# Hybrid decoder step on one core: cached keys turned by VectorE, their strips and the convolution's weights on two DMA queues

## What is computed

```
a = rmsnorm(h);  [q k v | h B C] = a @ w_in            # 8 heads x 64, conv 512
q, k = rmsnorm per head
att: distances in three patterns (window, step): (128,1), (512,4), (2048,16)
     prompt: banded attention; sample: one softmax over the strided keys
             of the cache (2048 rows) and the new ones, + T5 bias by distance
conv: u = C*h;  y = B * (w0*u[t-2] + w1*u[t-1] + w2*u[t])
h += [rmsnorm(att) | rmsnorm(y)] @ w_out
h += MoE(rmsnorm(h))      # 4 groups x 8 experts, top 1 group, top 2 experts
h += (p @ w_proj) * sigmoid(rmsnorm(h) @ w_gate)
```

## Time and profile before

| | us |
|---|---|
| median of 3 runs | 1082.3 (1080.84 to 1082.81) |
| profiled execution | 1082.67 |
| its span, first to last instruction | 1080.7 |
| convolution stage in it | 280 to 498 |

### The profile page before, as it was taken

One profiled execution on the slowest core, in us unless ns is written; L12 is line 12 of the kernel. 1 busy time (PEld: TensorE's weight loads), 2 busy tenths in 40 slices (PEclk: granted clock), 3 DMA queues, 4 the chain that ended last, 5 costly groups with the idle time before them and its releaser, 6 DMA issues.

```text
span 1080.7 us, 15684 instructions
## 1 busy us (share of the span) xinstructions
PE 1036.0 (96%) x5834; PEld 620.1 (57%) x5834; DVE 523.0 (48%) x1175; ACT 312.7 (29%) x665; POOL 212.4 (20%) x240
## 2 busy tenths in 40 slices
PE   7999999999999999999999999989999999889997
PEld 6888875565878777766555554334433333345443
DVE  6836634777733464545556464441111110047674
ACT  2332313777533322301111123111111111244331
POOL 0100001121433352531012111322231110130000
PEclk9999999999999999999999998989999999989999
DMA  9713214940563666663973237989999999974321
GB/s 315 190 31 116 71 50 119 293 101 6 215 213 112 212 211 216 207 244 81 355 270 128 94 105 280 405 340 414 418 410 410 419 420 399 371 288 157 119 78 78
DMA packets 99260, 242.11 MB, mean 224 GB/s; under 512 B 21206, under 2 KB 56958, under 8 KB 84528
## 3 DMA queue, kind: packets, MB, share of 16 engines
q1 hardware_dynamic: 88544, 212.10, 54.1%
q0 software_dynamic: 9920, 26.38, 6.4%
q10 hardware_dynamic: 720, 2.62, 0.6%
HBM read 210.12 MB, written 35.65 MB: 227 GB/s over the span
## 4 chain that ended last, share of the span: by engine, by line
PE 80%; DVE 6%; DMA 6%; SPq 4%; issue 2%; ACT 2%; POOL 0%; POOLq 0%; DVEq 0%; ACTq 0%
PE pair L2921 13%; PE pair L3124 13%; PE pair L2598 10%; PE pair L2976 9%; PE pair L3146 6%; PE pair L3228 5%; PE pair L3223 3%; PE pair L2739 2%; DMA h_dram<-R 2%; DMA R<-in_w_up 2%; PE pair L2713 2%; PE pair L3047 2%; PE pair L2755 2%; PE pair L3111 1%; SPq L707 1%
## 5 line engine op out<-in xcount | busy, mean ns | idle before, releaser
L2921 PE MATMUL pair<-R 128*128 128x264 f32 x672 | 160.2, 389 | 0.2 <-POOL R L1032 0.2
L3124 PE MATMUL pair<-R 128*32 128x512 f32 (+2 forms) x896 | 151.3, 601 | 5.2 <-DMA R<-in_w_up 3.0
L2598 PE MATMUL pair<-R 128*128 128x256 f32 x672 | 149.7, 382 | 0.4 <-DVE R L1755 0.4
L2598 PEld LDWEIGHTS pair<-R 128*128 128x128 f32 x672 | 127.0, 191 | 18.8 <-issue 1.0
L2921 PEld LDWEIGHTS pair<-R 128*128 128x128 f32 x672 | 123.5, 190 | 23.4 <-issue 3.5
L2976 PE MATMUL pair<-R 128*128 128x512 f32 x256 | 116.6, 606 | 0.0
L2329 DVE TENSOR_TENSOR R<-pair,R 128x256 f32<-128x256 f32 x21 | 8.9, 425 | 208.3 <-ACT R L1516 208.3
L3124 PEld LDWEIGHTS pair<-R 128*32 128x32 f32 (+2 forms) x896 | 48.8, 125 | 92.2 <-issue 87.8
L3146 PE MATMUL pair<-R,bias 128*32 128x512 f32 (+2 forms) x448 | 78.0, 611 | 2.7 <-issue 2.1
L2976 PEld LDWEIGHTS pair<-R 128*128 128x128 f32 x256 | 47.7, 192 | 53.3 <-issue 52.6
L3228 PE MATMUL pair<-R 128*128 128x512 f32 x168 | 73.0, 593 | 0.0
(11 more groups left out here) (366 smaller groups left out, 1471.5 us busy)
## 6 DMA issues: line engine op xcount, KB each, us to landing
R<-in_w_gate SPq DMA_DIRECT2D x32, 1024.0 KB, 12.3
R<-in_w_up SPq DMA_DIRECT2D x32, 1024.0 KB, 15.6
R<-in_w_down SPq DMA_DIRECT2D x32, 1024.0 KB, 16.8
R<-in_w_in SPq DMA_DIRECT2D x12, 1024.0 KB, 8.4
R<-in_x_prompt SPq DMA_DIRECT2D x16, 512.0 KB, 3.8
R<-in_cache_k SPq DMA_DIRECT2D x8, 1024.0 KB, 5.0
R<-in_cache_v SPq DMA_DIRECT2D x8, 1024.0 KB, 4.9
R<-y_dram SPq DMA_DIRECT2D x16, 512.0 KB, 5.9
```

What stands on the lines that cost most here:

```text
L2598: last = mm(qbank(p, part, k), lhs[:, c, :], rhs[:, c, :], start=(c == 0), stop=(c == 3))
L2921: last = mm(cbank(n, k), lhs[:, c, :], rhs[:, c, :], start=(c == 0), stop=(c == 3))
L3124: last = mm(bk[2 + u][r, :].rearrange("p (w f) -> p w f", w=2), xgT[u][:, c, r], wgu[s][:, :, c, :], start=(c == 0), stop=(c == DC - 1))
```

## The change

Key items are loaded in four strips of 32 partitions, so that a strip holds the rows of one quarter, and VectorE turns the keys in blocks of 32 x 32 into `kT` (16 blocks of 32 dimensions x 256 columns); TensorE no longer turns keys and ScalarE no longer copies them. A score row is now (head, quarter, token), so 128 rows x 256 columns hold one sequence, and a pass of the softmax covers two sequences instead of four: four passes, with the maximum and the sum taken over quarters by small transposes and reductions (`by_group`). The probabilities are turned by a multiplication with a reordered identity. The sample's q and k are turned in pieces of 32 x 32, and 16 copies during prompt attention arrange the queries (`q4`). Items are in a new order; SP loads strips 0 and 1 (for keys the near rows too), ScalarE's queue strips 2 and 3 of items 3 to 15 and the convolution's weights from the third group on. SP's `relbd` loads are one fourth as long and stand behind the first two `keep_xT`.

```diff
-ITEMS = [("k", b) for b in range(5)] + [("v", 0), ("k", 5), ("v", 1), ("k", 6), ("v", 2), ("k", 7)] + ...
+ITEMS = [("k", 0), ("k", 1), ("k", 2), ("v", 0), ("k", 3), ("v", 1), ("k", 4), ("v", 2),
+         ("k", 5), ("v", 3), ("k", 6), ("v", 4), ("k", 7), ("v", 5), ("v", 6), ("v", 7)]
+def sample_order():
...
+        parts += [*keys[0][0:1], ("norm", g - 1), *keys[0][1:2], ("turn", g - 1), *keys[0][2:4]]
+        if g < NPASS:
+            parts += [("score", 2 * g)]
+        parts += [("weigh", b), *keys[1][0:2], ("sum", b), ("weigh", b + 1), *keys[1][2:4]]
+        if g < NPASS:
+            parts += [("score", 2 * g + 1), ("soft", g)]
+        parts += [("sum", b + 1)]
+ROOM = {"key": 4, "score": 6, "soft": 2, "norm": 2, "turn": 4, "weigh": 8, "sum": 4}
...
+    def strip_rows(kind, b, kv, s):
+        strip, cache = slice(32 * s, 32 * s + 32), ck[b] if kind == "k" else cv[b]
+        far_rows = cache[0:512 * FARC, :].rearrange("(k r a) d -> a r k d", k=FARC, a=16)
+        if kind == "k":
+            return [(kv[strip, 4:7, :], far_rows[s])]
+        near = (kv[strip, 0:4, :], cache[PAST - NEAR:PAST, :].rearrange("(i r c) d -> c r i d", c=4, i=4)[s])
...
 # ScalarE
+        def load_strips(i):
...
+            for s in (2, 3):
+                for rows, src in strip_rows(kind, b, KV[i % 3], s):
+                    act.dma_start(rows, src).then_inc(S(f"ring_in{i % 3}"), 16)
+        def load_conv(n):
+            act.wait_ge(S("cv_full"), PRODUCTS * (n - 1))
+            act.dma_start(wC[n % 2], conv_weights(n)).then_inc(S(f"w_in{5 + n % 2}"), 16)
...
                 if k < KEPT_OF:
                     keep_product(n, k)
+                if k == 0 and 1 <= n < NCONV - 1:
+                    load_conv(n + 1)
...
+                for i in STRIPS_AT.get(at, ()):
+                    load_strips(i)
 # VectorE
+        def turn_keys(b, gg):
...
+            raw = kv[:, :, P * gg:P * gg + P].rearrange("p c (n x) -> p c n x", n=4)
+            out = kT[:, 4 * gg:4 * gg + 4, 0:PART].rearrange("p n (c r) -> p c n r", c=7)
+            dve.transpose(out[:, 0:4], raw[:, 0:4])
+            dve.transpose(out[:, 4:7], raw[:, 4:7]).then_inc(S("kt_done"), 1)
 # TensorE
-            for r in range(4):
-                last = pe.transpose(bk[4][:, P * r:P * r + P], kv[:, r, P * gg:P * gg + P], ident[:, :])
...
+            for hh in range(2):
+                for half in range(2):
+                    for j in range(NG):
+                        n = 4 * j + 2 * hh + half
+                        at = 32 * n + (0 if hh else 16)
+                        last = mm(out[strips[j], ROW * second:ROW * second + ROW], qbd_all[second][:, at:at + 32], kT[:, n, :], ...
...
+            for c in range(4):
+                last = mm(bk[4][:, P * c:P * c + P], Es[:, c // 2, P * (c % 2):P * (c % 2) + P], by_quarter, start=True, stop=True)
```

More of the change, by code:

```diff
@@ L67 @@
 SKN = SK + SAMP
+NPASS = NB // 2
+PART = SK // 4
+ROW = PART + SAMP
 CAP = 128
@@ L197 @@
[L197 to L206, removed]
@@ L207, with strip_loads @@
-ROOM = {"key": 4, "score": 4, "turn": 6, "weigh": 8, "sum": 4}
+    return i % 3, sum(ARRIVES[k] for k, _ in ITEMS[i % 3:i + 1:3])
+RING_USED = tuple(sum(ARRIVES[k] for k, _ in ITEMS[s::3]) for s in range(3))
+def strip_loads():
+    at = {}
+    for i in range(3, len(ITEMS)):
+        used, b = ITEMS[i - 3]
+        at.setdefault(place_of(("key", b, NG - 1) if used == "k" else ("weigh", b)) + 2, []).append(i)
+    return at
+def sample_order():
+    parts = []
+    for g in range(NPASS + 1):
+        keys = [[("key", 2 * g + d, gg) for gg in range(NG)] if g < NPASS else [] for d in range(2)]
+        if g == 0:
+            parts += keys[0] + [("score", 0)] + keys[1] + [("score", 1), ("soft", 0)]
+            continue
+        b = 2 * g - 2
+        parts += [*keys[0][0:1], ("norm", g - 1), *keys[0][1:2], ("turn", g - 1), *keys[0][2:4]]
[5 more added lines that the diff above has]
+        parts += [("sum", b + 1)]
+    return parts
@@ L224, with place_of @@
 PARTS_AT = spread_parts()
-def place_of(kind, b, gg=None):
-    return next(s for s, parts in PARTS_AT.items() for part in parts if part[0:2] == (kind, b) and (gg is None or part[2] == gg))
+def place_of(part):
+    return next(s for s, parts in PARTS_AT.items() if part in parts)
+STRIPS_AT = strip_loads()
 NSTAT = 6
@@ L803, in _ @@
         sp.dma_start(sel, I["c_sel"]).then_inc(S("small_in"), 16)
[L805 to L814, removed]
+        for i in range(3, len(ITEMS)):
+            load_item(i)
         sp.wait_ge(S("so_full"), 6)
@@ L2867, in weigh_values @@
             for k in range(FARC):
-                mm(bk[3][strips[k], :], rows(4 + k, P), KV[slot][:, 4 + k, :], start=False, stop=True)
-            last = mm(bk[3][strips[3], :], rows(7, P), V[:, PT, :], start=False, stop=True)
+                mm(bk[3][strips[k], :], PTs[:, second, 1, k, :], KV[slot][:, 4 + k, :], start=False, stop=True)
+            last = mm(bk[3][strips[3], :], PTs[:, second, 1, 3, :], V[:, PT, :], start=False, stop=True)
             last.then_inc(S("so_full"), 1)
@@ L2888, in sample_part @@
         def sample_part(kind, *more):
-            if kind == "key":
-                keys(more[0], more[1])
             if kind == "score":
```

377 lines of the change are left out of this document (195 added, 182 removed).

## The result

The changed kernel takes 1103.1 us (median of four runs, 1099.25 to 1107.22), the kernel before 1082.55 (1080.84 to 1084.18): the ratio is 1.0191, 95% interval 1.0150 to 1.0231. It is 1.9% slower; 1071 was forecast, range 1058 to 1085. The profiled execution took 1099.25 us, the shortest of the four, its span 1097.3.

The account below looks back on a forecast made before the run. TensorE, busy 96% of the span, was taken as the bound. Stage: 194.4 + 8.5 stalls + 3 weights = 205.9 against 218.0; with +1.3 outside, -10.8 from 1082.3 gives 1071.5, stated as 1071, range 1058 to 1085.

Parts of the forecast that it names:

- TensorE's sum, 194.4: Convolution stage by TensorE alone: 218.0 less 24.6 for key transposes and 1.1 for waits, plus 0.4 scores, 1.7 probabilities.
- VectorE's work, 162.5: VectorE's busy time in the convolution stage, from 113.6 us, with 39.7 for key turns; fits without much room.
- slow-turn rival: VectorE's key turns become the convolution stage's bound: gain gone at 2.24 us a part, kernel 1089 at 2.4; chance 0.15.
- the estimate of 2.18: Turning one key part on VectorE: seven times the Trainium skill's 311 ns, 2.18 us, against the 1.24 taken.
- I take 4 us of stall (0 to 8): Start of the convolution stage, until the second score: VectorE has about 34 us of work for 34 us of TensorE.
- 2.5 in all (0 to 4): Scores one slot after their last key turn: TensorE stalls 0.5 us in five of eight.
- 2 us: Last normalisation, sharing its slot with the turning of the probabilities: 5 us against two products' 3.6, a 2 us stall.
- The items have seven slots or more to land, 12 us; nothing: Key and value transfers in the convolution stage land in time, even at half rate; no cost taken.
- The weights' own term, 3 us: Convolution weights, issued later than before, make about four groups 1 to 2 us late: 3 us (0 to 20).
- late-strips rival: Values arrive 2 to 3 us late at each of eight weighings: 1089 to 1097; chance 0.04 together with others.
- Uncovered, 13 bursts x 1 us: Strip issues on ScalarE's queue, bursts of 2.5 us, delay copies of products; taken as nothing, 13 x 1 us if uncovered.
- Outside the stage, +1.3: Outside the convolution stage: start -0.7, sample transposes in attention +0.8, query copies +1.0, bias sums +0.2.

Follow-up runs that it names:

- g1: Changed kernel with turns before joins, weights issued earlier, nearly all transfers to 96 or 128 partitions, later scores and turnings, turned near keys written in runs of four: 1070.05 us.
- e2: Changed kernel with VectorE turning a slot's key part ahead of that slot's joins instead of behind them: 1094.7 us.
- e4: Changed kernel with all loads on the sync queue and the key turns ahead of the joins: 1100.1 us.
- e1: Changed kernel with strips 2 and 3 and the convolution's weights back on the sync queue: 1100.9 us.
- e9: Changed kernel with the earlier kernel's key and value transfers shared over two queues, so other rows are weighed: stage 228.0 us, whole 2223.8 us.
- e10: As e9, with the key turns ahead of the joins as well: stage 214.1 us, whole 2213.5 us.
- e3: Changed kernel with only 128 of the 896 columns of each key part turned, so scores are not those of the cache keys: 1099.1 us.

## Why the prediction was wrong

The sum said 205.9 us for the stage; it is 231.9, 26.0 more. Term by term:

- **TensorE's sum, 194.4: right within 1%.** g1 shows it without disturbance, 196.15 us at clock 1.00, 1.8 more. The largest mis-sized part was the score: from its start to the next product's 1.87 us (302.01 to 303.88) in place of 1.75, 1.0 us in eight.
- **VectorE's work, 162.5: near,** 154.8; turns 39.5 us against 39.7. The slow-turn rival (2.24 us a part) is wrong at 1.23, and with it the estimate of 2.18.
- **"I take 4 us of stall (0 to 8)", "2.5 in all (0 to 4)" and "2 us", sum 8.5: the step that failed.** Measured 22.2 us. The start was nearly right: 5.2 (1.8 to the first products, 1.06 and 2.30 at two scores). The other scores waited 8.3 (11.7 less 3.4) in place of 2.5, because the slots were taken as average ones; the 5.91 us fall in the slots with the second half's input differences, and where the joins ran beside GpSimd's sums. And all four normalisations share the place that I priced only for the last: three of them waited 3.85, 1.94 and 2.92 us.
- **The clock: a term that was not there.** From 280.84 to 512.73 TensorE was busy 205.5 us, 11.1 over the sum. g1 needs 196.2 for the same work at clock 1.00, so 1.8 are the sum's and 9.3 the clock's, as 0.96 of 232 us says too (9.3). The sum took waits at their own length, where each of the five longest, 18.2 us together, was followed by a stretch at the lower level.
- **"The items have seven slots or more to land, 12 us; nothing": wrong.** Values cost 3.3 us, and the slow strips filled every gap that another cure opened (7.6 to 17.8 us for sums in e2 to e4). The weights' own term, 3 us, was 0.9; that other waits covered the rest is argued from e2 to e4, not shown. The late-strips rival (1089 to 1097; eight waits of 2 to 3 us on top of 1071.5 would be 1088 to 1096) misses the time by 6 us, and its mechanism too: one weighing of eight waited, not all.
- **"Uncovered, 13 bursts x 1 us", taken as nothing: not separated.** Where ScalarE issued four strips the copy behind them came late (start, us, with the idle time before it):

```profile
305.97 2.62 ACTq L1446 DMA_DIRECT2D R<-in_cache_v  x4
308.69 0.39 ACT L1409 ACTIVATE R<-pair 128x264 f32<-128x264 f32 x1 [2.34 <-PE pair L2986]
```

  but e1, without the bursts, is not faster; it waits 9.3 us for sums instead, so it does not price them.
- **Outside the stage, +1.3:** the first product starts 0.8 us later; the gap of 0.83 us at the start is closed, as forecast (20.00 us busy from 40 to 60). After the stage 2.0 us are added (584.6 against 582.6). Neither is told from chance: in the experiments, e9 and e10 aside, the first product starts between 279.2 and 281.8 us, and the part after the stage takes 579.2 to 585.8.

Together 14.9 (waits: 26.4 against 8.5 + 3) + 11.1 + 1.4 (2.7 outside the stage against 1.3) = 27.4 of the 27.8 us between the 1071.5 of the sum and the profiled 1099.25; the other 0.4 is that the sum starts from the median before, 1082.3, and not from the profiled 1082.67. The median after lies 3.9 us higher still. The forecast's time was reached by g1, 1070.05, once turns, scores, normalisation and transfers stood where the sum had tacitly put them; that is another kernel, and its agreement to 1 us is partly luck, since its stage is 202.6 us where the sum had 205.9.

## What to carry to other kernels

When work moves to an engine that runs in order, its total tells little: follow the chain from what starts that engine in the densest group to what waits for it, and put the consumer further behind (here a score and a turning two or more products behind what they wait for). Add to a long wait what the lower clock may cost behind it: here 9.3 us on top of five waits of 18.2. A cure that moves no time (e3) need not be the wrong cure: look at which wait took the place, and undo two at once before a cause is dropped.

## What the runs showed of the hardware

- Writing a turned block with its elements 16 bytes apart costs VectorE 1.10 us for 512 columns; in runs of four elements 0.70, as with full runs. The Trainium skill (SBUF — State Buffer, the note on cachelines in "Door 1: The DMA port swizzle") gives lines of 16 bytes and a price for each new one, which agrees.
- While GpSimd formed its sums (3.92 of 4 us busy), VectorE's joins of 264 columns took 0.84 and 0.95 us (L2025, L2026, at 392.46), 0.43 at 336.60 without them; its turns kept 0.70 and 0.53 beside the sums. GpSimd is held up too: its sum at 394.71 took 1.73 us, the next, as VectorE turned, 0.72.
- The sample's eight transposes cost 0.61 us on TensorE; the 32 multiplications of 32 columns that took their place need hardly more:

```profile
198.85 0.75 PE L2729 MATMUL pair<-ident,R 32*32 32x32 f32 x64
199.54 0.66 PE L2855 MATMUL pair<-R 128*64 128x128 f32 x8
```

  0.69 us from start to start, where 1.4 was forecast from the earlier trace rows and 0.61 stands in the earlier trace rows.
